# The rest part of the fourth token sum moved by 64 bytes, and its product put first, in the Strassen halves of an MLP

## The reference, cut to what matters

```python
h = rms_norm(x, norm2_g[l]) * (1.0 + sc2) + sh2
x = x + g2 * (jnp.square(jax.nn.relu(h @ w_mlp1[l])) @ w_mlp2[l])
```

## Time and profile before

| what | value |
|---|---|
| median of three executions | 1156.21 us (1155.56 to 1156.94) |
| profiled execution, its own time | 1155.3 us |
| its span on the core | 1153.5 us |
| PE busy | 1116.0 us, 97% of the span |
| DVE busy | 981.2 us, 85% |
| ACT busy | 658.8 us, 57% |
| granted TensorE clock over the span | 0.989 |

### The profile page before, as it was taken

The page is one execution under the profiler, slowest core; times in us unless marked ns, Lnnn a source line. Parts: engine busy times, 40 slices in busy tenths (PEclk is TensorE's granted clock), DMA queues, the critical chain, the costliest instruction groups (busy, mean ns, idle before and its releaser), DMA issues.

```text
span 1153.5 us, 19470 instructions
## 1 busy us (share of the span) xinstructions
PE 1116.0 (97%) x7945; PEld 1029.0 (89%) x7945; DVE 981.2 (85%) x1213; ACT 658.8 (57%) x962; POOL 36.1 (3%) x52
## 2 busy tenths in 40 slices
PE   4999999999999999999999999999999999999996
PEld 4899999999887778999789999989999989999885
DVE  5998999988997998997888787988778988867685
ACT  6655448977775556545554445665445555455452
POOL 1000000000000000001000000000000000000000
PEclk6999999999999999999999999999999999999998
DMA  9999998878975798995555775588775688767441
GB/s 377 419 419 421 421 411 320 272 213 255 351 282 220 282 319 311 382 382 197 208 187 232 311 272 204 200 243 301 291 280 183 208 259 286 305 225 276 156 183 73
DMA packets 50832, 321.15 MB, mean 278 GB/s; under 512 B 6764, under 2 KB 8632, under 8 KB 14264
## 3 DMA queue, kind: packets, MB, share of 16 engines
q1 hardware_dynamic: 44592, 305.72, 69.0%
q0 software_dynamic: 4256, 11.55, 5.7%
q10 hardware_dynamic: 1896, 2.64, 0.8%
HBM read 305.20 MB, written 4.21 MB: 268 GB/s over the span
## 4 chain that ended last, share of the span: by engine, by line
PE 68%; DVE 16%; DMA 6%; ACT 5%; issue 4%; SPq 0%; ACTq 0%; DVEq 0%
PE quad L1342 12%; PE quad L1344 12%; PE quad L1343 12%; PE quad L1355 8%; PE quad L1357 8%; PE quad L1356 8%; DVE w_lo L1911 4%; DMA first_raw<-in_w_mod 3%; DVE mod_raw L1918 2%; PE quad L1401 2%; PE quad L1403 2%; PE quad L1402 2%; DVE first_raw L1918 2%; DMA y<-stage 2%; DMA mod_raw<-in_w_mod 2%
## 5 line engine op out<-in xcount | busy, mean ns | idle before, releaser
L947 ACT ACTIVATE w_hi<-raw 128x1024 fp32r<-128x1024 f32 (+1 forms) x332 | 344.1, 1042 | 253.6 <-PE quad L1344 163.1
L1911 DVE TENSOR_TENSOR w_lo<-raw,w_hi 128x1024 fp32r<-128x1024 f32 (+1 forms) x332 | 395.5, 1203 | 94.0 <-ACT w_hi L947 93.4
L1342 PE MATMUL quad<-act,w_hi 128*128 128x256 f32 x1528 | 426.7, 279 | 5.9 <-DVE w_lo L1911 3.8
L1343 PE MATMUL quad<-act,w_hi 128*128 128x256 f32 x1528 | 424.5, 278 | 0.0
L1344 PE MATMUL quad<-act,w_lo 128*128 128x256 f32 x1528 | 424.5, 278 | 0.0
L1342 PEld LDWEIGHTS quad<-act,w_hi 128*128 128x128 f32 x1528 | 288.1, 189 | 8.6 <-issue 4.6
L1343 PEld LDWEIGHTS quad<-act,w_hi 128*128 128x128 f32 x1528 | 289.4, 189 | 0.2
L1344 PEld LDWEIGHTS quad<-act,w_lo 128*128 128x128 f32 x1528 | 288.1, 189 | 0.0
L1355 PE MATMUL quad<-w_hi,u_hi 128*128 128x512 f32 x336 | 132.0, 393 | 1.1 <-DVE u_lo L2369 1.0
L1357 PE MATMUL quad<-w_hi,u_lo 128*128 128x512 f32 x336 | 131.1, 390 | 0.0
L1356 PE MATMUL quad<-w_lo,u_hi 128*128 128x512 f32 x336 | 130.7, 389 | 0.0
(11 more groups left out here) (369 smaller groups left out, 1699.6 us busy)
## 6 DMA issues: line engine op xcount, KB each, us to landing
raw<-in_w_main SPq DMA_DIRECT2D x184, 1024.0 KB, 6.2
mod_raw<-in_w_mod SPq DMA_DIRECT2D x67, 1024.0 KB, 7.8
first_raw<-in_w_mod SPq DMA_DIRECT2D x14, 1024.0 KB, 15.8
late_raw<-in_w_mod SPq DMA_DIRECT2D x10, 1024.0 KB, 8.1
acc<-in_w_mod SPq DMA_DIRECT2D x4, 1024.0 KB, 12.3
conv_b<-conv_q POOLq DMA_DIRECT2D x8, 512.0 KB, 5.6
y<-stage POOLq DMA_DIRECT2D x6, 512.0 KB, 8.9
shared<-stage POOLq DMA_DIRECT2D x6, 512.0 KB, 5.3
```

What stands on the lines that cost most here:

```text
L947: A(dst[:, 0:2 * width], block_half(raw, j, width), ACT.Copy).then_inc(hi_done, 1)
L1342: mm(out, hi, act_hi[:, k, :], start=begin and m % 2 == 0, stop=False, skip_group_check=True)
L1343: mm(out, hi, act_lo[:, k, :], start=False, stop=False, skip_group_check=True)
L1911: TTn(lo[:, 0:2 * width], block_half(raw, j, width), hi[:, 0:2 * width].bitcast(f32), ALU.subtract)\
```

## The change

The fourth token sum gets tensors of its own for its sum and its rest part, 64 bytes (`SHIFT` words) behind the place where they stood, so at 96 modulo 256; its hi part stays at 32. To make room, three allocations grow, and what follows them moves by 256, 512 or 768 bytes, so that its place modulo 256 stays. The ACT and DVE instructions that made the hi and rest parts of all four sums at once (128x512) become two each, of 384 and 128 columns. And the product with `s4` is issued as the first of the seven.

```diff
-        sb("last_sums", [P, 2 * GW])
-        last_sums_at = nc.sbuf_base - 8 * GW
+        sb("last_sums", [P, 2 * GW + 3 * BEAT // 4])
+        last_sums_at = nc.sbuf_base - 8 * GW - BEAT
...
+        s4_sum, s4_lo = ([nc.alloc_sbuf_tensor_at(f"s4_{part}{i}", [P, P], dt, offset=start + 4 * (GW + 3 * P + SHIFT))
+                          for i, start in enumerate(s_at)] for part, dt in (("sum", f32), ("lo", f32r)))
...
-                A(s_hi[i][:, :], s_sum[i][:, :], ACT.Copy).then_inc(s_cast, 1)
+                A(s_hi[i][:, 0:3 * P], s_sum[i][:, 0:3 * P], ACT.Copy)
+                A(s_hi[i][:, 3 * P:4 * P], s4_sum[i][:, :], ACT.Copy).then_inc(s_cast, 1)
...
-                s1, s3, s2, s4 = ((s_hi[j // 2][:, m * P:(m + 1) * P], s_lo[j // 2][:, m * P:(m + 1) * P])
-                                  for m in range(4))
+                s1, s3, s2 = ((s_hi[j // 2][:, m * P:(m + 1) * P], s_lo[j // 2][:, m * P:(m + 1) * P])
+                              for m in range(3))
+                s4 = (s_hi[j // 2][:, 3 * P:4 * P], s4_lo[j // 2][:, :])
...
                 pe.wait_ge(s_split, q * N_SPLIT + (j // 2 + 1))
+                product(plain[1], s4, b22)
                 product(mixed[0], a11, b11, first)
                 product(plain[0], a12, b21)
-                product(plain[1], s4, b22)
...
-                TTn(s_lo[i][:, :], s_sum[i][:, :], s_hi[i][:, :].bitcast(f32), ALU.subtract).then_inc(s_split, 1)
+                TTn(s_lo[i][:, 0:3 * P], s_sum[i][:, 0:3 * P], s_hi[i][:, 0:3 * P].bitcast(f32), ALU.subtract)
+                TTn(s4_lo[i][:, :], s4_sum[i][:, :], s_hi[i][:, 3 * P:4 * P].bitcast(f32), ALU.subtract).then_inc(s_split, 1)
```

More of the change, by code:

```diff
@@ L399, in build @@
         early_at = nc.sbuf_base - 4 * TT * GW
+        sb("early_spare", [P, BEAT // 4])
         conv_b = nc.alloc_sbuf_tensor_at("conv_b", [P, CT, S], f32, offset=early_at)
@@ L429, in build @@
         t_sum, t_hi, t_lo = split_parts("t", [mod_at + 4 * D * i for i in range(2)], 2 * GW)
-        s_at = [early_at, acc_at, acc_at + 8 * GW, last_sums_at]
+        s_at = [early_at, acc_at, acc_at + 8 * GW + BEAT, last_sums_at]
         s_sum, s_hi, s_lo = split_parts("s", s_at, GW)
+        s4_sum, s4_lo = ([nc.alloc_sbuf_tensor_at(f"s4_{part}{i}", [P, P], dt, offset=start + 4 * (GW + 3 * P + SHIFT))
+                          for i, start in enumerate(s_at)] for part, dt in (("sum", f32), ("lo", f32r)))
         u_keep = [nc.alloc_sbuf_tensor_at(f"u_keep{i}", [P, GW], f32, offset=start) for i, start in enumerate(s_at)]
@@ L2417, in token_sums @@
                 a11, a21, a12, a22 = (r4[:, k, tt * P:(tt + 1) * P] for k, tt in ((0, 0), (0, 1), (1, 0), (1, 1)))
-                s1, s3, s2, s4 = (s_sum[i][:, m * P:(m + 1) * P] for m in range(4))
+                s1, s3, s2 = (s_sum[i][:, m * P:(m + 1) * P] for m in range(3))
+                s4 = s4_sum[i][:, :]
                 link(TTn(s1, a21, a22, ALU.add))
```

## The result

The changed kernel takes 1166.79 us (median of 4, 1165.56 to 1168.17) against 1156.58 us before, a ratio of 1.0083 with a 95% interval of 1.0065 to 1.0101: 10 us slower, where 1154.6 us was predicted, with an upper end of 1157.2. The profiled execution has a span of 1163.8 us against 1153.5, 10.3 us more.

The account below looks back on a forecast made before the run. PE, busy for 97% of the span, was taken as the bound. Gains of 0.68, 0.73 and 0.25 us in quarters 0 to 2 summed to 1.66 us, taking the 1156.21 us median to 1154.6 us, range 1153.7 to 1157.2.

Parts of the forecast that it names:

- The place of `s4_lo`, with its product first: Strassen halves: a meeting at the second matmul brings 113.3 ns from the fifth on; about 0.085 us per half, 3.4 us for 40.
- The second rival: Strassen halves: no lasting effect, 117.8 ns stays or returns within a few matmuls; 1156.3 us, chance 0.37.
- its own terms of 0.08 and 0.2 us: In that rival: 0.08 us for the chain's longer DVE pair, perhaps 0.2 us for disturbed halves.
- What stands behind a half: After each Strassen half: only the ordinary half's gain of another 0.01 us was counted, with no term for up stages.
- The fourth rival: Strassen halves: the meeting throws each into a pace slower than 117.8 ns; 4.2 us, 1160 us, chance 0.07 (over 2.3 us).
- What of it reaches the end: Quarters 0, 1 and 2: 0.68, 0.73 and 0.25 us arrive, 1.66 us of 3.4, as waits take the rest.
- The chain: Quarter 2: ACT waits for DMA landings, DVE for ACT, PE for DVE; 21.54 us between landings against PE's 20.96.
- The signs: In the trace: halves about 2.40 us, PE waits about 1.2 us near 947 us and some 0.6 us near 776 us.
- The split instructions: DVE and ACT, 12 more instructions each: 0.08 us in quarter 2's chain, 0.6 at worst.
- Order and room: The `s4` product issued first and the moved allocations: no DMA or wait moves, cost 0.
- The rule on ports: PE's operand reads: the skill's independent ports would make place irrelevant; the prediction said the trace disagrees in part.

Follow-up runs that it names:

- e9: Changed kernel plus an unread matmul ahead of each up stage behind a Strassen half, and ACT's first stage copy one half earlier: 1153.44 us, ratio 0.9955.
- e11: Changed kernel with the `s4` product issued second in place of first: 1157.62 us, one execution.
- e1: Changed kernel with the `s4` product third, as before the change: 1156.06 us, ratio 1.0000.
- e4: Changed kernel with the fourth rest part for half 7 left at its old place, 32, in all groups: 1155.46 us, ratio 0.9980.
- e5: Changed kernel plus one unread matmul, a second meeting, ahead of each up stage behind a Strassen half: 1157.36 us, ratio 0.9988.
- e6: Kernel before the change plus one unread matmul ahead of each up stage behind a Strassen half: 1167.27 us, ratio 1.0080.
- e10: Kernel before the change plus two unread matmuls ahead of each up stage: 1156.61 us, one execution.
- e3: Kernel before the change with only the split instructions and grown allocations; place and product order as before: 1157.35 us, ratio 1.0009.
- e2: Changed kernel with the fourth sum and its rest part back at 32, new product order kept: 1157.93 us, ratio 1.0009.

## Why the prediction was wrong, point by point

**The place of `s4_lo`, with its product first.** Right in kind and size: 2.395 us a half for a predicted 2.40. The four matmuls were 118, 118, 119 and 113 ns instead of 118, 117, 122 and 116, and the sum of the half was met to 0.01 us. Together with the ordinary half behind it, a half gained 0.093 us (83.72 less 82.23 us in e9, over 16 halves) where 0.085 was forecast. The second rival, with a chance of 0.37, expected none of this; its own terms of 0.08 and 0.2 us add to 1156.5 us and not to the 1156.3 that it names. But the prediction was also lucky in where the product went. It carried over what a meeting does at a border, and nothing in that reasoning tells the second matmul of a half from the fifth or the eighth, where the same meeting changes nothing lasting (e11, e1).

**What stands behind a half.** This is the step that failed. The prediction costs the edit as "about 0.085 us for a half, 3.4 us for 40" and asks of each half only what the ordinary half behind it gains. Three of the 40 halves have an up stage behind them. The prediction used exactly this border as its evidence, "the 117.8 ns pace thus became the 113.3 ns pace over a border with a single such meeting", and didn't ask what the border does to a half that already runs at 113.3 ns. What the change does to the up stages was put at nothing. It measured 3.41 us for each of the three up stages, 10.2 us in all, against a gain of the halves that reached the end with less than 1 us (0.74 and 0.99 us in quarters 0 and 1, less 0.91 in quarter 2). e4 shows where it comes from: with no meeting in the half ahead of the border, the 10.2 us are gone. e5, e6 and e10 agree with an exchange by each meeting at the border, with the control above missing. The fourth rival named the other side and a size, but put it in the halves; they got shorter.

**What of it reaches the end.** In quarters 0 and 1 the sum said 0.68 and 0.73 us and the trace has 0.74 and 0.99. In quarter 2 it said 0.25 us of gain and the trace has a loss of 0.91. The chain was the right one, and e9 shows that it took the gain: with the same 40 short halves and no wait for a landing, the two quarters take 82.23 and 82.25 us, where the changed kernel has 82.73 and 85.02. The signs came in part. The wait of PE near 947 us was to grow to about 1.2 us, and it was 1.07; that of 0.6 us in quarter 1 didn't come near 776 us, but with 0.27 us one group earlier; and the 0.52 us at 932.01 us was not forecast. Mis-sized was the chain's steadiness: I took 21.54 us from one landing to the next from a single pair. The next pair of the same trace is 22.10 us apart (ACT's copies at 940.61 and 962.71 us), and in the changed kernel it is 22.57 (925.25 and 947.82), a difference larger than the whole gain of 0.25 us. ACT's longest wait for a landing was 4.59 us in place of 4.1.

**The split instructions.** 0.08 us predicted for the longer DVE pair, 0.06 measured; e3 shows no cost above the interval.

**Order and room.** Nothing that the halves or the up stages show, as predicted (e2, e3).

**The rule on ports.** The Trainium skill, "SBUF — State Buffer", section "Who interferes with whom", says that PE's two read ports are independent and PE never waits on anyone. By it the place of an operand could not matter. The changed kernel and e2 differ in that alone, with 2.395 and 2.477 us for a half and 90.46 and 87.05 us for an up stage, so the traces disagree with the rule as the prediction used it. That it is at these ports that the two reads disturb each other isn't shown.

## What to carry to other kernels

Where one shape of matmul has two distances between starts at one granted clock, the distance is a state that a stretch inherits: measure what each stretch inherits from the one before it, and cost an edit also by what it hands on, above all to the longest stretch behind it. A stretch that serves as evidence for a mechanism is also subject to it. And where a second chain runs close beside the bound, its reserve read from one execution is no budget; give its transfer room first (here by making one copy one half earlier), and then the gain arrives.

## What the runs showed of the hardware that I had not expected

- 256-column fp32r matmuls with a new weight load each run at 113.3 or 117.8 ns for as long as nothing disturbs them, more than 760 in a row, with the same instructions at the same addresses (the up stages of e1 and of the changed kernel).
- One matmul whose streaming operand and the load beside it have the same address modulo 256 (both at 96; other matmuls had 32 and 96) exchanges the two distances at the border from a Strassen half to an up stage. One, two and three of them alternate; that an added matmul without such a meeting would do nothing wasn't tested. Behind 512-column matmuls it sets the shorter distance as the second matmul of a half (2.395 us), and does nothing lasting as the fifth or eighth (2.483). Why the position matters stays open; no run tells.
- A 512 KB accumulating DMA landed in 5.4 us instead of 8.9 when it was issued one half earlier. What it met at the later point wasn't looked for.
